# A decoder step on one Trainium2 core: in the feed-forward blocks of the third token group, where the bank B sum stands in VectorE's order, and which engine adds the weights

## What is computed

```python
def conv_ffn(h, conv_prev, lp):
    B, T, _ = h.shape
    u = h @ lp['w_up']
    a, b = u[..., :D_FF], u[..., D_FF:]
    ext = jnp.concatenate([conv_prev.astype(a.dtype), a], axis=1)
    c = lp['conv_b'] + ext[:, 0:T] * lp['conv_w'][0]
    for j in range(1, CONV_W):
        c = c + ext[:, j:j + T] * lp['conv_w'][j]
    y = (jax.nn.gelu(c, approximate=False) * b) @ lp['w_down']
    return y, ext[:, T:]
...
xp, xs = x + f                      # then the final norm, and y
```

## Time and profile before

| what | value |
|---|---|
| median of 3 runs | 2822.91 us |
| lowest and highest run | 2814.49 and 2826.68 us |
| the profiled execution's own time | 2841.95 us |
| its span, first to last instruction | 2840.1 us |
| busy in the span: TensorE, VectorE, ScalarE, POOL | 2629.2, 1661.1, 765.0, 413.1 us |
| mean granted clock of TensorE | 0.959 of full speed |
| stage of the 34 blocks, in the span | from 2484 us to the end |

### The profile page before, as it was taken

One profiled execution on the slowest core, in us unless ns is written; L12 is line 12 of the kernel. 1 busy time (PEld: TensorE's weight loads), 2 busy tenths in 40 slices (PEclk: granted clock), 3 DMA queues, 4 the chain that ended last, 5 costly groups with the idle time before them and its releaser, 6 DMA issues. The chain is left out here.

```text
span 2840.1 us, 47722 instructions
## 1 busy us (share of the span) xinstructions
PE 2629.2 (93%) x18832; PEld 1739.1 (61%) x18832; DVE 1661.1 (58%) x3150; ACT 765.0 (27%) x1624; POOL 413.1 (15%) x525
## 2 busy tenths in 40 slices
PE   8998999999997977889799999999979999989897
PEld 5554566666653325778565666565646665588897
DVE  2116888855433466767489999778713322255655
ACT  2224322134434461111113331113335321121212
POOL 0000111000000000000002220002344420133432
PEclk9998999999998976999899999999989999999999
DMA  5101111231114330000352333353357543523332
GB/s 211 33 13 40 51 73 70 67 95 39 46 48 184 82 129 17 19 12 11 113 163 91 104 107 113 116 178 102 114 180 223 166 144 114 182 93 104 104 105 69
DMA packets 86207, 278.83 MB, mean 98 GB/s; under 512 B 18520, under 2 KB 42936, under 8 KB 72608
## 3 DMA queue, kind: packets, MB, share of 16 engines
q1 hardware_dynamic: 73952, 224.64, 23.7%
q0 software_dynamic: 12032, 51.14, 5.7%
HBM read 242.79 MB, written 32.16 MB: 97 GB/s over the span
## 5 line engine op out<-in xcount | busy, mean ns | idle before, releaser
L407 PE MATMUL dp_PS<-base,dp_W 128*128 128x368 f32 x1440 | 467.5, 477 | 0.0
L2167 PE MATMUL tl_P<-base,tl_WU 128*128 128x368 f32 x1408 | 447.1, 478 | 16.3 <-issue 11.2
L2167 PEld LDWEIGHTS tl_P<-base,tl_WU 128*128 128x128 f32 x1408 | 268.9, 192 | 186.8 <-issue 25.3
L407 PEld LDWEIGHTS dp_PS<-base,dp_W 128*128 128x128 f32 x1440 | 266.7, 191 | 158.3 <-issue 10.4
L2183 PE MATMUL tl_P<-base,tl_WD 128*128 128x368 f32 x704 | 223.1, 474 | 0.0
L148 PE MATMUL pa_PG<-pa_W,base 128*128 128x402 f32 (+1 forms) x576 | 199.1, 506 | 8.0 <-DMA pa_W<-in_w_dsa 8.0
L706 DVE TENSOR_SCALAR_CACHE_REDUCE dp_EQ<-dp_SCORE,dp_trial 128x1024 f32<-128x1024 f32 (+1 forms) x186 | 176.0, 946 | 19.9 <-issue 1.1
L2183 PEld LDWEIGHTS tl_P<-base,tl_WD 128*128 128x128 f32 x704 | 132.2, 190 | 83.2 <-issue 4.1
L148 PEld LDWEIGHTS pa_PG<-pa_W,base 128*128 128x128 f32 (+1 forms) x576 | 107.3, 187 | 94.9 <-issue 14.3
L2647 DVE MAX8 tl_v<-arena 128x8 f32<-128x4100 f32 x32 | 141.8, 4432 | 3.4 <-issue 1.5
L2594 POOL DMA_INDIRECT arena<-in_cache_kv,tl_PHT x128 | 122.7, 958 | 132.7 <-PE tl_P L2283 96.6
(11 more groups left out here) (447 smaller groups left out, 3994.6 us busy)
## 6 DMA issues: line engine op xcount, KB each, us to landing
tl_WU<-in_wu SPq DMA_DIRECT2D x58, 1024.0 KB, 4.9
tl_WD<-in_wd SPq DMA_DIRECT2D x32, 704.0 KB
dp_W<-in_w_rw SPq DMA_DIRECT2D x15, 1024.0 KB, 5.1
arena<-in_wb SPq DMA_DIRECT2D x24, 512.0 KB, 3.9
arena<-in_wo SPq DMA_DIRECT2D x24, 512.0 KB, 3.8
gates<-dp_PX SPq DMA_DIRECT2D x16, 552.0 KB, 3.4
arena<-gates SPq DMA_DIRECT2D x48, 184.0 KB, 3.9
arena<-in_wu SPq DMA_DIRECT2D x8, 1024.0 KB, 4.9
```

The costliest lines, as they stand in the source:

```text
L407: last = pe.matmul(bank(f)[:, 0:w], W[:, t // 2 % 2, k, 128 * (t % 2):128 * (t % 2) + 128], xT[:, k, c:c + w], start=k == 0, stop=k == KD - 1)
L2167: last = pe.matmul(out[:, 0:W], WU[:, i % 2, o:o + 128], XN[:, k, :], start=k == 0, stop=k == KD - 1)
```

## The change

`take2` is moved ahead of `multiply` in every block but the first down block of chunk 2, which needs the product at once. Weight sums 0 and 2 of blocks 1 to 33 are moved from POOL to VectorE, where all four sums now stand between `multiply` and `take3`; those of block 0 stay on POOL. A drain is added ahead of sums 1 and 3, and the sums of block 1 wait for POOL to have signalled those of block 0.

```diff
--- before.py
+++ after.py
@@ -1931,11 +1931,14 @@
 
         def weight_sum(eng, n, j):
             raw, ws = raw_at(n), sums_at(n)
+            if n == 1:
+                eng.wait_ge(sum_made[j], 1)
             if j in (0, 2):
                 eng.wait_ge(raw_in[n % 3], 16 * (n // 3 + 1))
                 if n >= 2:
                     eng.wait_ge(d_made, 2 * n - 2)
             else:
+                eng.drain()
                 eng.wait_ge(sum_made[j // 2 if j == 1 else 1], n + 1)
             if j == 0:
                 eng.tensor_tensor(ws[:, 0], raw[:, 2], raw[:, 3], ALU.add).then_inc(sum_made[0], 1)
@@ -2634,9 +2637,6 @@
                         keep_last(BLOCKS3[n - 1][1])
                     if BLOCKS3[n][0] == "up":
                         edge(BLOCKS3[n][1])
-                    if n + 1 < NBL:
-                        weight_sum(pool, n + 1, 0)
-                        weight_sum(pool, n + 1, 2)
                     right(n)
 
             @block.vector
@@ -2967,18 +2967,23 @@
                     total(2 * g + 1, KD - 1)
                     scale(2 * g + 1)
                 for n in range(NBL):
-                    if n and BLOCKS3[n - 1][0] == "up":
+                    after_up = n > 0 and BLOCKS3[n - 1][0] == "up"
+                    at_once = BLOCKS3[n] == ("down", 2, 0)
+                    if after_up:
                         convolve(BLOCKS3[n - 1][1])
-                        multiply(n - 1)
+                        if at_once:
+                            multiply(n - 1)
                     take2(n)
                     if BLOCKS3[n][0:2] == ("down", 2) and BLOCKS3[n][2]:
                         p = BLOCKS3[n][2] - 1
                         gain(p)
                         for t in (2 * p, 2 * p + 1):
                             total(5, t)
+                    if after_up and not at_once:
+                        multiply(n - 1)
                     if n + 1 < NBL:
-                        weight_sum(dve, n + 1, 1)
-                        weight_sum(dve, n + 1, 3)
+                        for j in (0, 1, 2, 3):
+                            weight_sum(dve, n + 1, j)
                     take3(n)
                     take_rest(n)
                 gain(3)
```

## The result

Median of four runs each: **2819.01 us before, 2773.66 us after** (2770.62 to 2775.63), a ratio of **0.9835, 95% interval 0.9808 to 0.9862**, 45.4 us less. The prediction was 2780, range 2769 to 2804.

A forecast was written before the change was run, and what follows sets the result against it. TensorE was taken to bound the block stage, waiting behind VectorE's take2. Waits 37.3, clock 4.8, chunk 2's first down block 1.2, its third -0.4: 42.9 us off the median 2822.91 gives 2780.0, range 2769 to 2804.

The forecast's parts named there:

- a restart cost of 0.235 us a gap: At TensorE's 21 waits behind take2, each gap costs some 0.235 us more than its recorded idle time.
- two times only: TensorE's waits behind take2 were said to have two recorded lengths, 0.73 and 2.32 us, in turn.
- VectorE's loop: VectorE's time for two blocks after the change, 16.69 us, under TensorE's 17.46, so TensorE remains the bound.
- a+2.78: a is the start of VectorE's last quarter's copy; take2 was predicted to start at a+2.74.
- The collision: Without POOL's sums, VectorE's two convolution steps take 1.32 us against 2.16, the product's first half 0.48 against 0.79.
- The sums' price: Four sums on VectorE take 2.81 us from the first sum to take3, with the added drains.
- the second rival: Sums on VectorE cost more in a row, 1.11 us each with a 0.42 gap: 2808 us; chance 0.05.
- The small places: Chunk 2's first down block wins 1.2 us; its third loses 0.4 us.
- The term "4.8": TensorE's clock falls at three places behind 2.3 us gaps, 1.6 us each; 4.8 us counted as won, bounds 0 and 4.8.
- the first: Rival: VectorE's convolution and product steps stay as long as they are, VectorE bounds: 2799 us; chance 0.06.
- the slower one: Rival: VectorE takes the up blocks' sums at POOL's pace, 1.59 us each: 2861 us; chance 0.03.
- the third: Rival: another TensorE wait of nearly the same size, such as bank B's release by take3, appears: 2815 to 2830; chance 0.05.

The follow-up runs named there:

- e3: Changed kernel, with POOL again computing two unused sums per block at the old place: 2793.69 us, ratio 0.9916 to the kernel before.
- e1: Kernel before with only take2 moved ahead of the gated product, sums left on POOL: 2780.16 us, ratio 0.986.
- e8: Changed kernel without the two drains added ahead of sums 1 and 3: 2798.12 us, one run.
- e5: Changed kernel once more, unedited, on another chip: 2798.41 us, ratio 0.9843 to the kernel before on that chip.
- e2: Kernel before with only the sums moved to VectorE, the product still ahead of take2: 2791.77 us, ratio 0.991.
- e4: Changed kernel with one more unused sum per block on VectorE: 2781.83 us, ratio 0.9867 to the kernel before.
- e10: Changed kernel with two more unused sums per block on VectorE: 2791.74 us, one run.

## Why the prediction was right

**The bound.** It read 21 waits behind take2 as the stage's loss, with a restart cost of 0.235 us a gap over the record. The stretch that holds them lost 42.40 us, 42.1 predicted (37.3 for the waits, 4.8 for the clock, which by the starts of the products was 5.0). One reading was too simple: "two times only" holds for 17 of the 21 waits, and the other four were 2.44, 1.80, 1.31 and 0.18 us. The sum went by the total, so nothing hung on it.

**VectorE's loop.** Predicted 9.14 us with a pair, 7.55 without, 16.69 for two. Measured 9.07 for the first; from that block's copy to the next take3 6.79, and 0.69 from take3 to the copy in the pair block, so 7.48: 16.55. Take2 stood at a+2.78 (2.74), the sums took 2.78 (2.81). Every term comes from a row that was there before the change; none was off by more than 0.1 us: 9.14 for 9.07 is the largest miss.

**The collision.** 0.62 + 0.08 + 0.62 = 1.32 us was taken for the convolution: 1.31 to 1.32. Product 0.48: 0.47. All 44 steps of the stage show it, as instructions of one line with least, middle and largest ns:

```profile
L2821 DVE SCALAR_TENSOR_TENSOR base<-tl_T,arena,base x44: 617/618/620, 2474.6 to 2728.3; 128x384 f32<-128x384 f32 x44
```

Before they were 617/1224/1534. With e3 the cause is shown: put POOL's work back, and 2.16 and 0.79 are back. By the Trainium skill (SBUF — State Buffer, Who interferes with whom) such a pair of instructions contends for one port pair under an exclusive lock. The runs agree that both sides pay: in the kernel before, POOL's sums take 1.42 and 1.59 us in up blocks and 1.27 in the down blocks without a convolution. Whether one shuts the other out for a whole instruction they don't show, as the records overlap (in e3 2500.07 to 2502.23 and 2500.33 to 2501.81). Nor is the price one number: e1 has 2.16 us in up blocks and 3.07 where both steps meet a sum. What the prediction left unsaid is that this price did not matter much here: e1 has it in full and lacks only 2.4 us.

**The sums' price.** Start distances 0.79, 0.61 and 0.78, none of the 0.42 us gaps of the second rival. The gap that the Trainium skill states (VectorE: DVE Perf Modes, The DRAIN you can't avoid) does not show in this kernel: a step of 0.69 us is followed after 0.61, behind a wait on its own result after 0.73 (e8), and with a drain as well after 0.79. The same section says that a next instruction which is not held starts earlier; the prediction left that out, and the 0.61 fits it.

**The small places.** Chunk 2's first down block: 1.21 won, 1.2 predicted (its convolution to product 1.97, 1.99 predicted). Its third: the next block's first product came 1.07 us behind the transposes' start in place of 0.65, so 0.42 lost, 0.4 predicted.

**What was off.** Two sizes, both of TensorE's clock. The term "4.8" was three falls of one execution (5.0 by start distances); another execution had four (6.7), so the term has a scatter of at least 1.7 us, which the bounds of 0 and 4.8 left out on the high side. And the prediction kept silent on the clock behind the wait that stays: there TensorE took 5.28 us for 18 matmuls in place of 4.28, 1.0 of the 1.49 lost at the end:

```profile
2731.90:2736.00 4.10, 4.09 (x13) 4.09 (x14) 1.59 (x4) 0.01 (x1) 0.00 (x0) 0.50 0.01 4
```

A granted clock of 0.50 is the lower of the two levels, 1.2 GHz, behind 4.6 us of idleness. In e5, the same kernel, these 18 took 4.38, so this is no effect of the change. The rest of the distance between 2780 and 2773.66 is largely the base: the median of before, from three runs then, is 2819.01 with a fourth; from it the prediction's difference gives 2776.1, 0.5 us over the highest of the four runs after. The stage's own 42.7 us in the traces is nearer to the 42.9 predicted than the medians' 45.4, which the runs' scatter leaves open.

That the range held is in part luck. Its terms give 2780 - 6 = 2774 at the low end, not the 2770 that is written, and no term stands for the 4 us between; the measured median is 2773.66. The prediction also took the whole profile's distance from the median, 19 us, for something outside the stage; that was right, but its reason (gaps of steady size) said nothing of what it was, and e5 had to show it.

**The 0.235 us of a gap.** The prediction inferred them from start distances alone. The rows say where they lie: the eight matmuls ahead of a gap have a record of 1.41 us where the next product would start after 1.25 (0.16), and the product behind a gap is followed after 1.33 (2537.14 to 2538.47) in place of 1.25 (0.08). Both are counted as busy. In e2 it holds again: ten gaps of 1.14 are 11.4 recorded and 13.7 with these, and the stage is 14.3 us longer than the changed kernel's.

**The rivals** all fell by the same rows: steps at 0.62 (the first), distances of 0.61 to 0.79 (the second and the slower one), no wait of TensorE behind L2864 or L2878 (the third). e3, e4 and e10 show how near they were: 1.2 us more of VectorE's work per pair is felt, 2.4 costs nearly half of the gain (18.7 and 19.1 of 42 us).

## What to carry to other kernels

When a fast engine waits for one step of a slower one, look first at what stands ahead of that step and could stand behind it: here swapping two steps gave 40 of 42 us, while making the steps ahead cheaper gave 28 by itself and 2.4 on top of it. Two remedies for one wait don't add, so try each alone before both. And compare stages, not spans: the two profiled executions differed by 66 us, a third of it ahead of the stage and none of the change's doing.

## What had not been expected of the hardware

- **Slow matmuls beside the gathers, by the chip.** On one chip (e5 to e8) TensorE issues 84 to 87 matmuls in the first 42.4 us of the third group's attention part, 90 in the first profile of before; in the other seven executions it is 211 to 238, and in both groups there are executions of the changed kernel. TensorE's rows name no engine that it waits for ("issue"), and POOL's indirect gathers run beside it in both. That costs some 23 us in all (415 to 417 us from there to the block stage, against 389 to 394). Why this chip does so stays open.
- **The clock falls only sometimes.** Behind gaps of 2.3 us, ten in each execution of before, it fell three times in one and four times in the other, only once at the same gap; behind the gaps of 1.8 us and less past the stage's fifth product never, in any of the twelve profiled executions. Once fallen it costs 1.7 us. Behind the waits of 4.6 us and more in chunk 2's first down block it fell every time, ten times in all, and 18 matmuls took 4.3 to 5.7 us in place of 2.81.
- **A collision's price differs with who starts first.** The same two convolution steps take 1.31 us without POOL's sums, 2.16 when the first sum starts some 0.3 behind them and 3.07 when it starts 0.15 ahead of them (e1).
- **Small lags are carried along.** With one sum more VectorE falls behind by 0.3 us a pair, and no wait is recorded until the chunk's end (e4). A wait in the profile can be the bill for blocks long past.
